# All moves of turned rows issued from GpSimd's queue in a one-core hybrid decoder layer

## The reference: what is computed

```python
x = x + 0.5 * _swiglu(_rmsnorm(x, ffn1_norm[l]), ffn1_w_gate[l], ffn1_w_up[l], ffn1_w_down[l])
u = _rmsnorm(x, mix_norm[l]) @ w_in[l]
...   # differential attention (4 heads) and stick-breaking attention (8 heads)
x = x + jnp.concatenate([a_out, b_out], axis=-1) @ w_out[l]
x = x + 0.5 * _swiglu(_rmsnorm(x, ffn2_norm[l]), ffn2_w_gate[l], ffn2_w_up[l], ffn2_w_down[l])
x = _rmsnorm(x, final_norm[l])
# _swiglu(x, g, u, d) = (silu(x @ g) * (x @ u)) @ d ; hidden width D_FF = 5632
```

## Time and profile before

| | us |
|---|---|
| median of three runs | 1829.8 |
| the profiled execution | 1829.58 |
| its span | 1827.8 |
| PE busy in it | 1815.4 |
| DVE busy | 1320.1 |
| ACT busy | 936.7 |
| POOL busy | 21.7 |

### The profile page before, as it was taken

One profiled execution on the slowest core, in us unless ns is written; L12 is line 12 of the kernel. 1 busy time (PEld: TensorE's weight loads), 2 busy tenths in 40 slices (PEclk: granted clock), 3 DMA queues, 4 the chain that ended last, 5 costly groups with the idle time before them and its releaser, 6 DMA issues.

```text
span 1827.8 us, 22094 instructions
## 1 busy us (share of the span) xinstructions
PE 1815.4 (99%) x8332; PEld 1506.9 (82%) x8332; DVE 1320.1 (72%) x1545; ACT 936.7 (51%) x1168; POOL 21.7 (1%) x19
## 2 busy tenths in 40 slices
PE   9999999999999999999999999999999999999998
PEld 7888888888888888888888888888888888888887
DVE  7888558887568868656666566888558887678865
ACT  7554434554345545555666445554434554345554
POOL 0000000000000000100000000000000000000000
PEclk9999999999999999999999999999999999999998
DMA  9565655556646647655554466665655556556653
GB/s 339 199 217 195 212 191 190 199 197 237 214 142 226 221 161 245 214 169 167 168 188 163 159 216 234 199 216 195 213 190 191 199 197 242 201 201 224 218 171 113
DMA packets 233922, 367.01 MB, mean 201 GB/s; under 512 B 16368, under 2 KB 94960, under 8 KB 233840
## 3 DMA queue, kind: packets, MB, share of 16 engines
q1 hardware_dynamic: 232352, 364.05, 59.3%
q10 hardware_dynamic: 1488, 1.87, 0.3%
HBM read 346.85 MB, written 2.10 MB: 191 GB/s over the span
## 4 chain that ended last, share of the span: by engine, by line
PE 98%; DVE 1%; SPq 0%; DMA 0%; issue 0%; ACT 0%; POOL 0%; DVEq 0%
PE psum L1814 74%; PE psum L1855 11%; PE psum L1727 7%; PE psum L1732 3%; PE psum L1836 1%; SPq L466 0%; DVE strip_sum L1238 0%; DVE squares L1230 0%; PE psum L1978 0%; PE psum L1989 0%; PE psum L2024 0%; PE psum L2004 0%; DVE x_res L1676 0%; DMA w_raw<-in_ffn_gate 0%; PE psum L1694 0%
## 5 line engine op out<-in xcount | busy, mean ns | idle before, releaser
L1814 PE MATMUL psum<-w_split,x_split 128*128 128x512 f32 x3792 | 873.9, 390 | 0.0
L1814 PEld LDWEIGHTS psum<-w_split,x_split 128*128 128x128 f32 x3792 | 710.6, 188 | 150.3 <-DVE w_split L1055 0.6
L724 ACT ACTIVATE w_split<-w_raw 128x1024 fp32r<-128x1024 f32 (+2 forms) x400 | 399.0, 1013 | 351.4 <-PE psum L1814 253.7
L613 ACT ACTIVATE w_split<-w_raw 128x1024 fp32r<-128x1024 f32 (+1 forms) x340 | 348.5, 1040 | 361.6 <-PE psum L1814 296.2
L1055 DVE TENSOR_TENSOR w_split<-w_raw,w_split 128x1024 fp32r<-128x1024 f32 (+1 forms) x340 | 400.0, 1199 | 172.5 <-ACT w_split L613 170.9
L1196 DVE TENSOR_TENSOR w_split<-w_raw,w_split 128x1024 fp32r<-128x1024 f32 (+2 forms) x400 | 452.0, 1163 | 89.0 <-ACT w_split L724 87.8
L1814 PE MATMUL psum<-w_split,h_split 128*128 128x512 f32 x2208 | 503.1, 389 | 0.2 <-DVE h_split L1273 0.2
L1814 PEld LDWEIGHTS psum<-w_split,h_split 128*128 128x128 f32 x2208 | 413.9, 188 | 87.7 <-DVE w_split L1196 1.3
L1855 PE MATMUL psum<-w_split,pair_sums 128*128 128x512 f32 x480 | 127.9, 395 | 0.0
L1855 PEld LDWEIGHTS psum<-w_split,pair_sums 128*128 128x128 f32 x480 | 90.1, 188 | 21.7
L1855 PE MATMUL psum<-w_split,x_split 128*128 128x512 f32 x360 | 96.2, 393 | 0.0
(11 more groups left out here) (211 smaller groups left out, 930.5 us busy)
## 6 DMA issues: line engine op xcount, KB each, us to landing
w_raw<-in_ffn_down SPq DMA_DIRECT2D x76, 1024.0 KB, 5.3
w_raw<-in_ffn_up SPq DMA_DIRECT2D x67, 1024.0 KB, 5.4
w_raw<-in_ffn_gate SPq DMA_DIRECT2D x66, 1024.0 KB, 7.9
w_raw<-in_w_in SPq DMA_DIRECT2D x48, 512.0 KB, 5.0
w_raw<-in_w_in SPq DMA_DIRECT2D x24, 1024.0 KB, 5.2
w_raw<-in_ffn_gate SPq DMA_DIRECT2D x42, 512.0 KB, 4.1
w_raw<-in_ffn_up SPq DMA_DIRECT2D x40, 512.0 KB, 4.9
w_raw<-in_w_out SPq DMA_DIRECT2D x16, 1024.0 KB, 5.2
```

The lines of the kernel that those rows point to most:

```text
L613: nc.scalar.activation(w_split[:, slot % 2, 0, h * half:(h + 1) * half], w_raw[:, slot, h * half:(h + 1) * half], ACT.Copy).then_inc(hi_ma ...
L724: nc.scalar.activation(w_split[:, n % 2, 0, part[0]:part[1]], w_raw[:, slot, part[0]:part[1]], ACT.Copy).then_inc(hi_made, 1)
L1814: ins = mm(psum[:, bank + t, :], x[:, a, t * P:(t + 1) * P], w[:, b, k, :], start=kk == 0 and (a, b) == (0, 0) and t in begins, stop=kk == ...
```

## The change

GpSimd's program gets the moves, in the order in which they are needed, between its powers. SP's program loses every `move_turned` and the table `moves` that placed them; ACT's loses `move_last_quarter`. A move on GpSimd waits for `hidden_32` and for the reader of the move before (`free`), and then issues all 16 DMAs.

```diff
         @block.sync
-                        if j == 5 and i:
-                            move_turned(ph["moved"] + i)
-                        if i == 0:
-                            for count in moves.pop(2 * ph["s0"] + j, ()):
-                                move_turned(count)
...
-                def move_turned(count, quarters=4):
-
-                    sp.wait_ge(hidden_32, count)
-                    for q in range(quarters):
-                        for a in range(4):
-                            sp.dma_start(hidden_moved[32 * q:32 * q + 32, a, :, :, :], turned_32[32 * a:32 * a + 32, q, :, :, :]).then_inc(
-                                hidden_landed, 16)
...
         @block.gpsimd
+            def move_turned(free):
+
+                moved["count"] += 1
+                pool.wait_ge(hidden_32, moved["count"])
+                if moved["free"] is not None:
+                    pool.wait_ge(*moved["free"])
+                for q in range(4):
+                    for a in range(4):
+                        pool.dma_start(hidden_moved[32 * q:32 * q + 32, a, :, :, :], turned_32[32 * a:32 * a + 32, q, :, :, :]).then_inc(
+                            hidden_landed, 16)
+                moved["free"] = free
+
+            def moves_of(ph):
+                if ph["kind"] == "ffn_in":
+                    n = ph["bodies"] - (not ph["all_moved"])
+                    for i in range(n):
+                        move_turned((hidden_ready, ph["g0"] + i + 1))
+                elif ph["kind"] == "wide" and ph["turns"]:
+                    for i in range(3 + (ph["norm"] is None)):
+                        move_turned((res_done, ph["r0"] + i + 1))
...
             norm_rstd(0)
+            for ph in phases[:mix_at]:
+                moves_of(ph)
             norm_rstd(NORM_MIX)
...
             out_power(1)
+            moved["free"] = (diff_ready, 2)
+            moves_of(phases[mix_at + 1])
             norm_rstd(NORM_FFN2)
+            for ph in phases[mix_at + 2:]:
+                moves_of(ph)
...
         @block.scalar
-            def move_last_quarter(count):
-
-                act.wait_ge(hidden_32, count)
-                for a in range(4):
-                    act.dma_start(hidden_moved[96:128, a, :, :, :], turned_32[32 * a:32 * a + 32, 3, :, :, :]).then_inc(hidden_landed, 16)
-
             def wide(ph):
...
-                        elif i + q == 0:
-                            move_last_quarter(ph["last_moved"])
                         hi_parts(c, c // 4, c % 4, ph["kn"])
```

More of the change, by code:

```diff
@@ L428, in _ @@
         def _(sp):
-            moves = {}
             for ph in phases:
@@ L498, in wide_chunks @@
                         sp.dma_start(dst, source(i, q)).then_inc(landed[c % 4], 16)
-                        for count in moves.pop(c, ()):
-                            move_turned(count, 3 if ph["g0"] is not None and ph["all_moved"] and count == ph["last_moved"] else 4)
                     if ph is phases[3]:
                         move_tables(i)
-                    if ph["turns"] and (i < 3 or ph["norm"] is None):
-                        moves.setdefault(2 * ph["s0"] + ph["chunks"] * (i + 1) + 4, []).append(ph["moved"] + i + 1)
                 def four_chunks(i):
@@ L551, in _ @@
                         group_chunks(i)
-                if ph["kind"] == "ffn_in" and ph["all_moved"]:
-                    moves[2 * ph["s0"] + 8 * ph["bodies"] + 4] = [ph["moved"] + ph["bodies"]]
-                elif ph["kind"] == "wide":
+                if ph["kind"] == "wide":
                     for i in range(4):
@@ L576, in norm_rstd @@
                 power(rstd_tok[:, :], mean_sq[:, 0:2], norm_power)
+            moved = {"count": 0, "free": None}
+            def move_turned(free):
[16 more added lines that the diff above has]
+                        move_turned((res_done, ph["r0"] + i + 1))
+            mix_at = next(n for n, ph in enumerate(phases) if ph["kind"] == "mix")
             norm_rstd(0)
+            for ph in phases[:mix_at]:
+                moves_of(ph)
             norm_rstd(NORM_MIX)
```

## The result

The changed kernel takes 1855.86 us (median of four runs, 1854.07 to 1859.01) against 1829.8 us before; the ratio is 1.0145, with a 95% interval of 1.0133 to 1.0157. It is 26 us slower where I had forecast 53. Direction and main place of the loss, the four ends, are as predicted. The two numbers that the forecast was built of, d and L, are both wrong, in opposite directions: with the right d alone I would have forecast no change, so the sign is partly luck.

The account below looks back on a forecast made before the run. PE was taken as the bound, busy 1815.4 of 1827.8 us. Ends 31.8, FFN2's x 9.3, FFN1's x 7.0 and clock 5 summed to 53 us on 1829.6, giving 1883 us; range 1836 to 1932.

Parts of the forecast that it names:

- the four ends: Ends of parts, where PE needs the moved fourth hidden group: late moves were to stop PE for 31.8 us in all.
- d: Time of one DMA issue on GpSimd, 16 per move: taken as 1.0 us, with 0.75 to 1.25 as the forecast's band.
- L: Time from a move's last issue to its reader's start: 1.27 us on SP, taken as 1.5 on GpSimd.
- the limits of M: Longest harmless time from a move's first issue to its reader's start at the ends: 9.50, 9.68, twice 9.5 us; 38.2 together.
- The slope that I gave: Sensitivity to issue time: 0.1 us more per issue costs 6.4 us at the ends, 16 us together.
- what the change removes: On SP, 464 issues go and weight loads come earlier; ACT loses four issues per end: worth nothing for the time.
- my second rival, "not slower": At the ends, GpSimd issues in 0.5 us or less, so moves arrive in time: 1829.4 to 1829.8 us, chance 0.12.
- The x moves: Moves of x that DVE adds late: 9.3 us in FFN2's second `wide`, 7.0 us in FFN1's third.
- my limit of 14.4: In FFN2's second `wide`, the longest time in us from an x move's first issue to DVE's add without PE waiting.
- The clock: After each of the four stops, the first matmuls run at 1.2 GHz: 1.2 us each, 5 us in all.
- GpSimd held up by DVE: GpSimd's issues wait for running DVE operations, raising issue time by 0.4 to 1.4 us: 1965 us; chance 0.18 including other causes.
- Nothing at the end of the program: After the last result: the prediction's sum had no term for the program's end.

Follow-up runs that it names:

- e1: The changed kernel, with SP holding its next weight loads at the four ends until the end move has landed: 1833.33 us, ratio 1.002.
- e7: The kernel before, with only the ten moves of x (160 transfers) issued from GpSimd: 1831.06 us, ratio 1.0008.
- e5: The changed kernel, with the four end moves given back to SP (12 issues) and ACT (4), the other 26 on GpSimd: 1829.70 us, ratio 1.0.
- e3: The kernel before, with all 16 issues of each of the four end moves on ScalarE, none from SP or GpSimd: 1863.22 us, ratio 1.0185.

## Why the prediction was half right

**What bounds the kernel, and where it breaks: right.** PE was the bound, the four ends were where a move can be late, and the limits of M (38.2 us together) held within some 0.3 us each. Measured M of 52.5 less 38.2 is 14.3, and PE waited 14.7 us. In e1 PE waited only at the two ends with the longest M, 0.2 us at 9.64 and 0.4 at 9.85.

**The issue, d = 1.0 us: wrong by a factor of two.** It is 0.496. I took the middle between SP's issue, 0.59, and POOL's power, 1.36 in the median. SP's row, the same operation, was 0.1 off; the row of POOL was another kind of work and should have had little weight. This is the term that made the forecast twice too large: 16 issues took 8 us less per move than I had said, and L took 3.8 us of that back at the ends. The slope that I gave, 6.4 us at the ends for 0.1 us of d, shows how much hung on it. The Trainium skill's figure (DMA: Bandwidth & Descriptors, Specifications), 1 us to the first byte from GpSimd against 0.6 from SyncE, isn't a price of issuing: here the queue moves on after 0.496 us, and a piece lands after 1.7 us, as from SP.

**What follows the issue, L = 1.5 us: wrong by a factor of three to four.** It is 4.5 to 5.6 us. The failed step is the sentence on what the change removes: SP's "weight loads come earlier. That is worth nothing in the end". I asked who would profit from an earlier load, found nobody, and put it at zero. I did not ask whom it would hurt. I even named the loads beside the move's last rows, and added 0.23 us for them. The trace of before could have said more: in the 8.9 us of the first end's move the DMA engines were busy for 0.22 of the time, in the changed kernel for 0.64 (the same columns as in the stretches above; before, then after).

```profile
181.70:190.60 8.90, 8.90 (x40) 7.13 (x39) 6.61 (x7) 4.08 (x5) 0.00 (x0) 1.00 0.22 59
```

```profile
181.70:190.60 8.90, 8.90 (x40) 7.08 (x39) 6.59 (x7) 3.18 (x3) 7.82 (x16) 1.00 0.64 206
```

The Trainium skill has the rule (DMA: Bandwidth & Descriptors, Queues, rings and completion order): each DMA engine takes turns between the queues that have work for it, so a queue of its own is no DMA engine of its own. The runs agree, 1.7 us alone and 4.5 to 5.6 beside loads, and from ACT's queue 1.9 alone and 4.5 beside the first load.

**The errors cancel in part.** The ends were forecast at 31.8 us and cost 14.5. With L as before, 16 x 0.496 + 1.27 would be 9.2 us, below every limit, and the time that of before: my second rival, "not slower", decided at d = 0.51. Its condition on d was met and it failed all the same, by L. With my d and the true L, which is 5.3 in the mean and so 3.8 us more in each M, the sum would be an estimated 1883 + 15 = 1898. The slowdown that I foresaw came about through a mechanism that I had dismissed.

**The x moves, 9.3 and 7.0 us: wrong, with d.** At M near 9.5 they are early enough. FFN2 shows one late add, its first, where the loads run beside the move again:

```profile
1577.93 20.14 SPq L482 DMA_DIRECT2D w_raw<-in_ffn_down  x4
...
1582.51 7.81 POOL L564 DMA_DIRECT2D lo_sum<-head_out  x16 [23.51 <-issue]
...
1594.12 1.29 DVE L1352 TENSOR_TENSOR x_res<-lo_sum,x_res 128x512 f32<-128x512 f32 x2 [6.57 <-DMA lo_sum<-head_out]
...
1596.69 3.68 PE L1812 MATMUL psum<-w_split,h_split 128*128 128x512 f32 x15 [0.62 <-DVE w_split L1053]
```

M is 11.6 here against 11.27, with 3.8 of it behind the last issue, but the move is the 25th on GpSimd and starts 3.4 us after its transposes end at 1579.12. So the add comes 15.0 us after the transposes. Before, the move followed them at once, so my limit of 14.4 counts from there: 0.6 us too late, and PE waits 0.62. In e7, where the ninth move is the third of this phase, it is 15.5 us after them (1602.15 to 1617.62), and PE waits 1.10. The limit was right; the cost came from a late start that I did not foresee, and where it falls is a matter of the count. At FFN1's moves of x PE does not wait, and e5, where all ten are on GpSimd and neither the ninth, the 17th nor the 25th move is in FFN2's `wide`, has a ratio of 1.0.

**The clock, 5 us: right in kind, 6.2 to 7.0 in size.** A stop of 3 us is followed by 3.4 us at half the clock; I had allowed 2.4.

**GpSimd held up by DVE (0.18 of the chance): wrong.** The longest of 480 issues took 0.689 us, at a DVE that is busy for 71% of the span. The page of the Trainium skill that I named for it (SBUF — State Buffer, Who interferes with whom) has the exception for operations with two inputs; the trace goes with the exception.

**Nothing at the end of the program: wrong.** 2.45 us, which are in no part of the sum. I looked for waits inside the body and took the end for given.

## What to carry to other kernels

When a transfer leaves a queue, look at what the queue does in the time that it gains, and at what that runs beside: a load that comes earlier and helps nobody can still delay the transfer that somebody waits for, here by 3.3 to 4.3 us. A queue of its own takes away waiting to be issued, not waiting for the DMA engines; hold the large loads back until the urgent small transfer has landed, which here gave back 22.5 of 26 us. A stop of some 3 us of TensorE costs half as much again in clock, and an engine that issues its first DMAs can become the last one to finish the program.

## What the runs showed of the hardware that I had not expected

- Issuing a DMA of 32 rows of 1 KB takes 0.496 us on GpSimd, 0.591 on SyncE and 0.64 on ScalarE (e3, 10.24 for 16).
- Such a DMA lands after 1.7 to 1.9 us alone. Beside loads of 1 MB it lands after 4.5 to 5.6 us from GpSimd's queue; from ScalarE's, beside one such load, after 4.5 and then 2.9.
- GpSimd's drain at the end of the program is 1.91 us plus 1.31 us for each 16 DMAs, counted from 1 to 8 and then from 1 again: 12.4 us after 128, 4.5 after 160. The first DMA behind each full 128 begins some 3.1 us later than others do. Of the drain only what lies beyond the landing of the last output (6.5 to 6.9 us after GpSimd's last instruction here) is paid.
- After a stop of 3.0 us, TensorE's clock was at 1.2 GHz for 3.4 us, beginning 0.8 us after it was busy again; in the stops of 3.93 and 3.97 us it fell some 0.5 us before that. Filled with dummy matmuls, the first stop kept it at 1.00.
